# Attention latents projected with tokens as rows, normalised at the PSUM exit, and moved ahead of the SSM inputs

## The reference

```python
proj = h @ w_in[l]
c_q, c_kv, k_pe, u_ssm, conv_a, conv_g = jnp.split(proj, IN_SPLITS, axis=-1)
# mla_mixer
q = (rms_norm(c_q, q_a_norm) @ w_uq).reshape(B, L, N_HEADS, QK_HEAD)
kv = (rms_norm(c_kv, kv_a_norm) @ w_ukv).reshape(B, L, N_HEADS, QK_NOPE + V_HEAD)
# rms_norm
y = xf * lax.rsqrt(jnp.mean(xf * xf, -1, keepdims=True) + eps)
return (y * w.astype(jnp.float32)).astype(x.dtype)
```

## Time and profile before

| | us |
|---|---|
| median of three runs | 1255.36 |
| the profiled execution | 1256.61 |
| its span in the trace | 1254.5 |
| TensorE busy | 1130.0 |
| VectorE busy | 978.3 |
| ScalarE busy | 700.2 |
| POOL busy | 378.5 |

### The profile page before, as it was taken

One profiled execution on the slowest core, in us unless ns is written; L12 is line 12 of the kernel. 1 busy time (PEld: TensorE's weight loads), 2 busy tenths in 40 slices (PEclk: granted clock), 3 DMA queues, 4 the chain that ended last, 5 costly groups with the idle time before them and its releaser, 6 DMA issues.

```text
span 1254.5 us, 15926 instructions
## 1 busy us (share of the span) xinstructions
PE 1130.0 (90%) x5636; PEld 866.9 (69%) x5636; DVE 978.3 (78%) x1182; ACT 700.2 (56%) x818; POOL 378.5 (30%) x359
## 2 busy tenths in 40 slices
PE   4899999688888889996699999999999999999992
PEld 3447565555666568785588888888887887787771
DVE  1979999846655646367799999999998998899971
ACT  5521225544454643223377777777777777777751
POOL 2304007376854000011212233332333333243220
PEclk9999999899999999997799999999999999999996
DMA  6700000000005000337599999999999999999930
GB/s 198 169 0 1 0 10 18 2 0 1 2 1 231 5 34 2 123 129 272 216 388 366 370 395 373 394 400 377 380 383 380 372 364 366 373 355 369 362 129 10
DMA packets 55485, 260.93 MB, mean 208 GB/s; under 512 B 31089, under 2 KB 31761, under 8 KB 41617
## 3 DMA queue, kind: packets, MB, share of 16 engines
q1 hardware_dynamic: 45344, 243.03, 50.5%
q0 software_dynamic: 10096, 17.34, 5.7%
HBM read 252.25 MB, written 26.35 MB: 222 GB/s over the span
## 4 chain that ended last, share of the span: by engine, by line
PE 60%; DVE 19%; DMA 9%; issue 4%; ACT 4%; SPq 2%; POOL 0%; DVEq 0%; ACTq 0%; POOLq 0%
PE psum L2112 26%; PE psum L2132 11%; DMA w<-in_w 9%; PE psum L2024 6%; DVE arena L1305 6%; DVE arena L1107 5%; PE psum L1972 3%; PE psum L1942 2%; PE psum L1758 2%; PE psum L1960 2%; PE psum L2102 2%; DVE am L1435 1%; PE psum L2118 1%; PE psum L1928 1%; DVE arena L1110 1%
## 5 line engine op out<-in xcount | busy, mean ns | idle before, releaser
L1602 DVE TENSOR_TENSOR w_rest<-w,w_high 128x2048 fp32r<-128x2048 f32 x136 | 305.3, 2286 | 18.3 <-ACT w_high L1028 18.0
L1028 ACT ACTIVATE w_high<-w 128x2048 fp32r<-128x2048 f32 x136 | 256.4, 1913 | 73.0 <-DMA w<-in_w 52.8
L2112 PE MATMUL psum<-w_high,xgT_high 128*128 128x512 f32 x544 | 217.5, 400 | 12.2 <-DVE xgT_rest L1648 12.1
L2112 PE MATMUL psum<-w_rest,xgT_high 128*128 128x512 f32 x544 | 213.7, 393 | 0.0
L2112 PE MATMUL psum<-w_high,xgT_rest 128*128 128x512 f32 x544 | 213.3, 392 | 0.0
L1655 DVE TENSOR_TENSOR w_rest<-w,w_high 128x2048 fp32r<-128x2048 f32 x68 | 152.5, 2284 | 1.8 <-ACT w_high L1038 1.8
L1038 ACT ACTIVATE w_high<-w 128x2048 fp32r<-128x2048 f32 x68 | 126.3, 1908 | 20.3 <-DMA w<-in_w 20.2
L691 POOL DMA_INDIRECT out<-arena,idx x34 | 91.7, 2697 | 123.6 <-DVE arena L1668 118.3
L2112 PEld LDWEIGHTS psum<-w_high,xgT_high 128*128 128x128 f32 x544 | 102.9, 189 | 37.2 <-issue 14.3
L2112 PEld LDWEIGHTS psum<-w_rest,xgT_high 128*128 128x128 f32 x544 | 102.9, 189 | 22.0
L2112 PEld LDWEIGHTS psum<-w_high,xgT_rest 128*128 128x128 f32 x544 | 103.1, 190 | 20.4
(11 more groups left out here) (269 smaller groups left out, 2032.0 us busy)
## 6 DMA issues: line engine op xcount, KB each, us to landing
w<-in_w SPq DMA_DIRECT2D x102, 2048.0 KB, 18.0
arena<-in_x SPq DMA_DIRECT2D x5, 1024.0 KB, 4.9
h_scratch<-arena SPq DMA_DIRECT2D x8, 512.0 KB, 2.6
out<-arena SPq DMA_DIRECT2D x8, 512.0 KB, 3.6
arena<-in_x SPq DMA_DIRECT2D x1, 3072.0 KB, 20.5
arena<-in_w_in SPq DMA_DIRECT2D x1, 2688.0 KB, 14.9
arena<-in_w_in SPq DMA_DIRECT2D x1, 2048.0 KB, 12.3
wout_y_raw<-in_w_out SPq DMA_DIRECT2D x1, 2048.0 KB, 9.9
```

The source lines that it names most:

```text
L1028: act.activation(w13h[k][:, c, :], w13[b][k][:, c, :], ACT.Copy).then_inc(W13H_READY[k], 1)
L1602: dve.tensor_tensor(w13l[b][k][:, c, :], w13[b][k][:, c, :], w13h[k][:, c, :].bitcast(F32), S_).then_inc(W13_SPLIT[k], 1)
L2112: last = pe.matmul(psum[:, k, :], x_[:, c, :], w_[:, c, :], start=(c == 0 and n == 0), stop=(c == KC - 1 and n == 2))
```

## The change

The latents are projected tile by tile with the tokens as rows, query and key/value latent side by side in one bank (128x384, sixteen passes a tile). ScalarE squares both out of PSUM with a row sum (the mean, since 1/sqrt(n) is in the scale), POOL adds eps and takes the power -1/2 for the two columns of the tile, and ScalarE copies the latents out of PSUM multiplied by that. TensorE turns the copies back, twelve 128x128 blocks for four tiles, and ScalarE saves the turned blocks to `cqT` and `ckvT`. All of this stands ahead of the SSM inputs, but that the second half is turned behind two of their tiles. The squares in SBUF, the products by ones and the scales in the q, k and v copies are gone. POOL's scaling of the q and kv weights stands behind the eight latent powers. The buffers `latt` lie where x tiles were and where `utok` will be.

```diff
--- before.py
+++ after.py
@@ -129,8 +129,9 @@
         Braw = at(YT0 + 1024, 2, NPAIR, C)
         kst = at(YT0 + 1280, NT, RD)
         sigT = at(19772, 2, T)
-        sqc = at(14336, 3, T)
+        latt = [at(S0 + 4096 + (QL + KL) * i if i < 3 else S0 + (QL + KL) * (i - 3), QL + KL) for i in range(NT)]
         cacc = at(YT0 + 2048, 2, T)
+        squares_q, squares_k = at(YT0 + 1024, QL), at(S0 + 1920, KL)
         wukv = at(48192, H * (ND + VD))
         tmp = at(49216, 1024)
 
@@ -315,10 +316,10 @@
 
         F_XT = lambda i, k: 2 * i + k + 4 * (2 * i // NT)
         F_AG = lambda half, m: (NT + 4) * half + NT + m
-        F_U = lambda i: 2 * NT + 8 + i
-        F_LAT = lambda half, m: 3 * NT + 8 + 3 * half + m
-        F_SSQ = 3 * NT + 14
-        F_QKV = lambda i, k: F_SSQ + 1 + 4 * i + k
+        F_LAT = lambda i: 2 * NT + 8 + i + (3 if i >= 6 else 0)
+        F_U = lambda i: 3 * NT + 11 + i + (3 if i >= 2 else 0)
+        F_TURN = lambda half, m: (2 * NT + 14 if half == 0 else 3 * NT + 13) + m
+        F_QKV = lambda i, k: 4 * NT + 14 + 4 * i + k
 
         R_C, R_W, R_H, R_U, R_V, R_CONV, R_Y, R_Z, R_GLU = range(9)
 
@@ -586,13 +587,15 @@
                     v = natural(upad[:, m, TAPS - 1:PADW], half)
                     pool.tensor_tensor(v, v, natural(sigT[:, m, :], half), ALU.mult).then_inc(upad_ready, 1)
             pool.wait_ge(wproj_in, 16 * 3)
+            for i in range(NT):
+                pool.wait_ge(lat_squared, i + 1)
+                mean, root = st[:, 16 + 2 * i:18 + 2 * i], st[:, 32 + 2 * i:34 + 2 * i]
+                link(pool.tensor_scalar(root, mean, 1.0, EPS, ALU.mult, ALU.add))
+                pool.tensor_tensor(root, root, minus_half[:, 0:2], ALU.pow).then_inc(lat_rms, 1)
+
             for c in range(2):
                 pool.tensor_scalar(wuq[:, c, :], wuq[:, c, :], normc[:, 2 * KC + c:2 * KC + c + 1], None, ALU.mult)
             pool.tensor_scalar(wukv, wukv, normc[:, 2 * KC + 2:2 * KC + 3], None, ALU.mult).then_inc(wproj_scaled, 1)
-
-            pool.wait_ge(lo_drained, F_SSQ + 1)
-            rms(16, 32, QL, NT, EPS, lat_rms)
-            rms(24, 40, KL, NT, EPS, lat_rms)
 
             def square_qk(i):
                 pool.wait_ge(qk_saved, i + 1)
@@ -818,8 +821,34 @@
             last.then_inc(hi_drained, 1)
 
             act.wait_ge(ssm_w_ready, 1)
+
+            def save_latents(i):
+                bank = lo(F_LAT(i))
+                act.wait_ge(lo_filled, F_LAT(i) + 1)
+                act.activation(squares_q, bank[:, 0:QL], ACT.Square, scale=QL ** -0.5, accum_out=st[:, 16 + 2 * i:17 + 2 * i])
+                act.activation(squares_k, bank[:, QL:QL + KL], ACT.Square, scale=KL ** -0.5,
+                               accum_out=st[:, 17 + 2 * i:18 + 2 * i]).then_inc(lat_squared, 1)
+                act.wait_ge(lat_rms, i + 1)
+                act.activation(latt[i][:, 0:QL], bank[:, 0:QL], ACT.Copy, scale=st[:, 32 + 2 * i:33 + 2 * i])
+                act.activation(latt[i][:, QL:QL + KL], bank[:, QL:QL + KL], ACT.Copy,
+                               scale=st[:, 33 + 2 * i:34 + 2 * i]).then_inc(lo_drained, 1)
+
+            def save_turned(half):
+                act.wait_ge(upad_ready, 4)
+                for m in range(3):
+                    n = F_TURN(half, m)
+                    act.wait_ge(lo_filled, n + 1)
+                    dst = cqT[:, m, :] if m < 2 else ckvT
+                    act.activation(natural(dst, half), lo(n).rearrange("p (i j) -> p i j", i=4), ACT.Copy).then_inc(lo_drained, 1)
+
+            for i in range(NT):
+                save_latents(i)
+                if i == 5:
+                    save_turned(0)
             for i in range(NT):
                 n = F_U(i)
+                if i == 2:
+                    save_turned(1)
                 act.wait_ge(lo_filled, n + 1)
                 act.activation(kst[:, i, :], lo(n)[:, 0:RD], ACT.Copy)
                 act.activation(utok[:, :, i, :], lo(n)[:, RD:RD + SW].rearrange("p (g c) -> p g c", c=C),
@@ -834,35 +863,18 @@
                 last = act.activation(U[:, 4 * k:4 * k + 4, :], psum[:, 4 + k, :].rearrange("p (g j) -> p g j", g=4), ACT.Copy)
             last.then_inc(hi_drained, 1)
 
-            act.wait_ge(upad_ready, 4)
-            for half in range(2):
-                for m in range(3):
-                    n = F_LAT(half, m)
-                    act.wait_ge(lo_filled, n + 1)
-                    dst = cqT[:, m, :] if m < 2 else ckvT
-                    act.activation(natural(dst, half), lo(n).rearrange("p (i j) -> p i j", i=4), ACT.Copy).then_inc(lo_drained, 1)
-            act.wait_ge(lo_drained, F_LAT(1, 2) + 1)
-            for m in range(3):
-                last = act.activation(sqc[:, m, :], cqT[:, m, :] if m < 2 else ckvT, ACT.Square)
-            last.then_inc(lat_squared, 1)
-            act.wait_ge(lo_filled, F_SSQ + 1)
-            act.activation(st[:, 16:16 + 2 * NT], lo(F_SSQ)[:, 0:2 * NT], ACT.Copy).then_inc(lo_drained, 1)
-
-            act.wait_ge(lat_rms, 2)
-
             def save_qkv(i):
                 for k in range(2):
                     n = F_QKV(i, k)
                     act.wait_ge(lo_filled, n + 1)
-                    act.activation(qraw[:, i, k * 384:k * 384 + 384], lo(n)[:, 0:384], ACT.Copy,
-                                   scale=st[:, 32 + i:33 + i]).then_inc(lo_drained, 1)
+                    act.activation(qraw[:, i, k * 384:k * 384 + 384], lo(n)[:, 0:384], ACT.Copy).then_inc(lo_drained, 1)
                 for k in range(2):
                     n = F_QKV(i, 2 + k)
                     act.wait_ge(lo_filled, n + 1)
                     v = lo(n).rearrange("p (h d) -> p h d", d=ND + VD)
                     for dst, d0 in ((kraw, 0), (vtok, ND)):
                         last = act.activation(dst[:, i, k * 256:k * 256 + 256].rearrange("p (h d) -> p h d", d=ND),
-                                              v[:, :, d0:d0 + ND], ACT.Copy, scale=st[:, 40 + i:41 + i])
+                                              v[:, :, d0:d0 + ND], ACT.Copy)
                     link(last)
                     act.sem_inc(lo_drained, 1)
                 act.sem_inc(qk_saved, 1)
@@ -1789,7 +1801,28 @@
             last.then_inc(hi_filled, 1)
 
             pe.wait_ge(win_scaled, 1)
+
+            def project_latents(i):
+                bank = lo(F_LAT(i))
+                for c in range(KC):
+                    last = pe.matmul(bank[:, 0:QL + KL], hT[:, c, i, :], win[:, c, CQ0:KPE0], start=(c == 0), stop=(c == KC - 1))
+                last.then_inc(lo_filled, 1)
+
+            def turn_latents(half):
+                pe.wait_ge(lo_drained, F_LAT(4 * half + 3) + 1)
+                for m in range(3):
+                    bank = lo(F_TURN(half, m))
+                    for i in range(4):
+                        last = pe.transpose(bank[:, i * P:(i + 1) * P], latt[4 * half + i][:, m * P:(m + 1) * P], ident[:, :])
+                    last.then_inc(lo_filled, 1)
+
             for i in range(NT):
+                project_latents(i)
+                if i == 5:
+                    turn_latents(0)
+            for i in range(NT):
+                if i == 2:
+                    turn_latents(1)
                 bank = lo(F_U(i))
                 for c in range(KC):
                     last = pe.matmul(bank[:, 0:RD + SW], hT[:, c, i, :], win[:, c, KPE0:A0], start=(c == 0), stop=(c == KC - 1))
@@ -1808,9 +1841,6 @@
             for g in range(G):
                 last = pe.transpose(psum[:, 4 + g // 4, (g % 4) * P:(g % 4 + 1) * P], utok[:, g].rearrange("p t c -> p (t c)"), ident[:, :])
             last.then_inc(hi_filled, 1)
-            for half in range(2):
-                for m, c0 in enumerate((CQ0, CQ0 + P, CKV0)):
-                    project(F_LAT(half, m), half, c0)
             hi(R_V)
             for k in range(2):
                 for r in range(NPAIR):
@@ -1819,13 +1849,7 @@
                                          WT[:, k, r, h * S:(h + 1) * S], U[:, 2 * r + h, :], start=True, stop=True)
             last.then_inc(hi_filled, 1)
 
-            pe.wait_ge(lat_squared, 1)
-            bank = lo(F_SSQ)
-            for i in range(NT):
-                for m in range(2):
-                    pe.matmul(bank[:, i:i + 1], sqc[:, m, i * P:(i + 1) * P], ones[:, 0:1], start=(m == 0), stop=(m == 1))
-                last = pe.matmul(bank[:, NT + i:NT + i + 1], sqc[:, 2, i * P:(i + 1) * P], ones[:, 0:1], start=True, stop=True)
-            last.then_inc(lo_filled, 1)
+            pe.wait_ge(lo_drained, F_TURN(1, 2) + 1)
             pe.wait_ge(wproj_scaled, 1)
 
             def project_qkv(i):
```

## The result

The changed kernel takes 1316.34 us (median of 4 runs, 1312.42 to 1319.85), the kernel before in the same comparison 1255.41: a ratio of 1.0478, 95% interval 1.0445 to 1.0511. The forecast was 1260 with a range up to 1264. Its sign was right, its size was not: +61 us in place of +4.7. The profiled execution took 1314.61 us with a span of 1312.5 (before 1256.61 and 1254.5), so the profile shows 58 us of the loss.

What follows compares the result with a forecast made beforehand. VectorE's serial work from 94 to 237 us was taken to bound the kernel, with V becoming the last thing it needs. +3.9 (V) +1.3 (clock) -0.5 (squares) = +4.7 on the median 1255.36 gave 1260, range 1254.3 to 1264.0.

Steps and rivals of the forecast that it cites:

- A wait that the banks make: TensorE before latent tile 6 waits until tile 5's bank is drained through ScalarE, POOL, ScalarE: 3.2 us (1.6 to 4.3).
- POOL's part: POOL's scale and power for latent tile 5, including waits for VectorE's step borders: 2.6 us (1.0 to 3.2).
- rival 3: POOL's small operations and weight scalings hold VectorE in the convolution, VectorE 11.5 us late: 1266 us; chance 0.08.
- What goes: Removed one-column products and POOL powers, some 11 us with TensorE and ScalarE little busy: gain nothing, covered by VectorE's serial work.
- The stall: TensorE stands idle between the first turns and latent tile 6: 3.2 us (1.6 to 4.3).
- V: TensorE's 32 matmuls (L1818) that VectorE's first rotation reads: ready 12.8 us after H's start, at 187.2; +3.9 us.
- H: TensorE's product at L1803, behind the SSM input projections, before U is turned: starts at 174.4.
- The clock: TensorE falls to the 1.2 GHz level for part of latent tile 6 after its idle gap: +1.3 us.
- The squares: POOL's squares of q and k come earlier, falling partly on VectorE products that read PSUM: -0.5 us (0 to -3.4).
- The scaling of the weights: POOL's scaling of wuq and wukv moves: convolution starts 2.6 us earlier, about 2.6 comes back inside it; net zero.
- the sum: Over the whole kernel: +3.9 (V), +1.3 (clock), -0.5 (squares), making +4.7 us.

Runs made afterwards that it cites:

- change healed: Changed kernel, convolution pausing at every second step up to step 34, q/kv weight scaling and q, k squares of tiles 0 and 1 on ScalarE: 1256.97 us, ratio 1.0028.
- weights: Kernel before, with the q and kv weights (wuq, wukv) scaled on ScalarE instead of POOL: 1258.39 us, ratio 1.0014.
- pause: Changed kernel, with every second VectorE convolution step waiting for its own predecessor: 1258.83 us, ratio 1.0048.
- raw: Changed kernel, latents copied unscaled, scales in q, k, v copies, one 16-column POOL scale and power, weight scaling in its old place; result not right: 1259.28 us, ratio 1.0040.
- pause 8: Changed kernel, with VectorE's convolution waiting for its own last step at every eighth step only: 1262.14 us (one run).

## Why the prediction was wrong, point by point

- *The failed step* stands in "A wait that the banks make": "POOL also waits for VectorE ... The convolution gives a border every 1.196 us ... POOL's part is 2.6 (1.0 at the least, 3.2 at the most)". It took one copy that slipped in at a border between two VectorE operations as the rule for 58 of them. Those two were the first with both inputs in SBUF behind one that reads PSUM, as VectorE's line ahead of them shows:

```profile
712.97 1.22 DVE L1648 TENSOR_TENSOR xgT_rest<-psum,xgT_high 128x1024 fp32r<-128x1024 f32 x1 [0.42 <-ACT xgT_high L1000]
```

Measured in place of the 2.6: 2.3 and 1.9 us for the second and the third tile, 62.5 for the fourth. The term was 60 us too small; its upper end was an assumption about the mechanism and not a bound.
- *The Trainium skill*, in "SBUF — State Buffer", section "Who interferes with whom", says that a VectorE instruction with two SBUF inputs contends with a POOL instruction that reads SBUF, not with one that only writes. The runs agree as far as they go: beside steps with one SBUF input the scale takes 0.19, beside steps with two it is held for 60.19; a memset took 0.10 where a read took 1.24. Its other rule is that whoever issues first holds the pair for its whole instruction. I read it as letting POOL in behind at most one step; 60.19, 61.07 and 42.53 us show that the loser can go on losing. I weighed the rule only for what POOL costs VectorE (rival 3), not for what VectorE costs POOL.
- *Rival 3* fell: POOL's small operations never held the convolution (69.44 in the changed kernel, and nothing beyond the pauses in `change healed`).
- *"What goes", taken at nothing: right.* In `change healed` ScalarE stood idle for 6.68 us before the square root, released by VectorE, so the earlier q, k and v gained nothing there. But the margin is thin, as `weights` showed.
- *The stall:* forecast 3.2, measured 2.28 and 2.27 with the hold gone, 1.33 with POOL at free speed. POOL's part, forecast 2.6, was 1.9 in `pause` (128.02 to 129.93: 0.22 for the scale, 1.61 for the power).
- *V:* forecast 12.8 us after H's start; 245.12 less 230.74 is 14.4, of which 1.7 is the lower clock in V; 12.7 in `change healed`. H came at 173.62 in `pause`, against 174.4.
- *The clock:* forecast +1.3, with the stall. Measured 0 in `pause` (10.59 for tiles 6 and 7) and 1.7 in `change healed` (12.28) with the same stall of 2.3. Both ends occur.
- *The squares:* forecast -0.5. From the rotation's start to the end of the six products it was 23.47 before, 22.78 in `raw` and 22.34 in `pause`: -0.7 and -1.1.
- *The scaling of the weights:* 2.6 for the convolution's start was right (106.74 against 109.19 for its two-input steps is 2.5). That it "comes back inside the convolution" was right as well wherever POOL is let in: 2.1 us in `pause` and in `pause 8`. In the changed kernel itself the scaling is queued behind the held scale and runs at 200.27, after the convolution.

Without the failed term the sum comes near, in part by luck. In `pause` it was +4.2 between the medians (1258.83 against 1254.68; by the ratio +3.4 to +8.8), but only +2.2 between the two profiled executions (1258.79 against 1256.61). In these the rotation starts 3.46 us later (186.78; forecast 3.9), the clock costs nothing (forecast 1.3) and the squares give 1.1 (forecast 0.5). And V alone doesn't make the 3.46: the convolution, longer by pauses and scaling, is ready within 0.3 us of V.

## What to carry to other kernels

Before a small POOL operation is put on a path that others wait for, look at what VectorE runs beside it: a long row of operations with two SBUF inputs and no wait between them kept POOL's reads out of SBUF until the row was over or in its last step, and a read of two columns fared no better than one of sixteen. Give such a row a wait for its own last result every eight operations (0.12 us each here), or put the small work on ScalarE, beside PSUM-reading operations, or where nobody waits. One pair of operations that was seen does not bound the cost for a long row: where two engines take turns, ask whether the waiting side ever wins.

## What the runs showed that I had not expected

- The hold has an onset: POOL is let in until about 5.5 two-input instructions after VectorE last stood still and is held from 7.8 on, by count and not by time. A single wait for the own predecessor ends it, at a price of 0.12 us, whether it stands at every 16th, eighth or second step.
- POOL's larger operations are another matter: once let in, the scaling of the weights cost the convolution 2.1 us.
- VectorE pays nothing for holding POOL (69.44 both times), and a POOL power that is let in beside the steps takes 1.61 in place of 0.69.
- Making VectorE's part of the path shorter made the kernel no faster, because it moved its scans onto POOL's powers; with VectorE's own work reordered as well, there was a gain.
